# Dealing the experts' contraction rows so that each partition reads one contiguous 16 KB piece of every gate, up and down matrix

## The reference

```python
def moe_ffn(h, g_norm, wgr, bgr, wer, ber, wg, wu, wd):
    u = rms_norm(h, g_norm).reshape(n, d)                 # n = 264, d = 1024
    gates = route(u, wgr, bgr, wer, ber)                  # two of 16 experts per token, others 0
    a = jnp.einsum('td,edf->tef', u, wg)                  # wg, wu: (16, 1024, 512) per layer
    c = jnp.einsum('td,edf->tef', u, wu)
    hh = jax.nn.silu(a) * c * gates[:, :, None]
    return h + jnp.einsum('tef,efd->td', hh, wd)          # wd: (16, 512, 1024) per layer
```

## Time and profile before

| | |
|---|---|
| median of 3 runs | 1362.0 us (1359.39 to 1366.07) |
| the profiled execution | 1360.1 us, of which the span of the trace is 1358.3 us |
| busy: TensorE matmul | 1150.4 us, 85% of the span |
| busy: TensorE weight load | 741.9 us, 55% |
| busy: VectorE, ScalarE, GpSimd | 421.2, 224.3 and 222.5 us |
| mean granted TensorE clock | 0.911 |
| DMA | 462.63 MB, mean 341 GB/s; SP's queue 88.5% of the 16 engines' span |

### The profile page before, as it was taken

How to read it: one execution, slowest core, us unless ns; L and a number is a source line. 1 busy time by engine, 2 the same in 40 slices (tenths; PEclk the granted TensorE clock), 3 DMA queues, 4 the chain that set the end, 5 groups by cost and what they waited for, 6 DMA issues and landing times.

```text
span 1358.3 us, 15981 instructions
## 1 busy us (share of the span) xinstructions
PE 1150.4 (85%) x5409; PEld 741.9 (55%) x5410; DVE 421.2 (31%) x821; ACT 224.3 (17%) x508; POOL 222.5 (16%) x466
## 2 busy tenths in 40 slices
PE   0899899999969999857898989888466989899888
PEld 0588688788723788744444444444354444444443
DVE  0354745845810575140111011112741111111112
ACT  0122122122100343111111111111011111111111
POOL 0002412411410121004012222100003122222100
PEclk9899999999967799965999999999665999999999
DMA  9999899999789988999999898998999898989997
GB/s 310 309 339 344 295 392 370 376 403 369 285 299 379 357 257 282 345 371 332 359 373 350 331 348 334 356 390 329 384 325 303 309 366 313 351 334 350 385 340 278
DMA packets 132562, 462.63 MB, mean 341 GB/s; under 512 B 12112, under 2 KB 20192, under 8 KB 129808
## 3 DMA queue, kind: packets, MB, share of 16 engines
q1 hardware_dynamic: 118768, 440.29, 88.5%
q0 software_dynamic: 5536, 18.88, 3.8%
q10 hardware_dynamic: 8232, 3.13, 1.0%
HBM read 455.19 MB, written 183.41 MB: 470 GB/s over the span
## 4 chain that ended last, share of the span: by engine, by line
PE 58%; DVE 8%; issue 5%; ACT 2%; POOL 1%; ACTq 1%; DMA 0%; POOLq 0%; DVEq 0%
PE bank L1192 17%; PE bank L1175 11%; PE bank L1208 8%; PE bank L1217 4%; PE bank L1130 2%; PE bank L1062 2%; PE bank L1089 1%; PE bank L1182 1%; PE bank L1109 1%; PE bank L1097 1%; PE bank L1139 1%; PE bank L278 1%; PE bank L1069 1%; PE bank L1086 1%; DVE scratch L929 1%
## 5 line engine op out<-in xcount | busy, mean ns | idle before, releaser
L1019 PE MATMUL bank<-uT,ring_lo 128*128 128x264 f32 x1152 | 275.0, 394 | 8.5 <-DVE uT L291 6.0
L1019 PEld LDWEIGHTS bank<-uT,ring_lo 128*128 128x128 f32 x1152 | 218.7, 194 | 49.2 <-issue 9.6
L1175 PE MATMUL bank<-scratch 128*128 128x128 f32 (+1 forms) x768 | 149.2, 328 | 40.3 <-POOL scratch L559 24.8
L1175 PEld LDWEIGHTS bank<-scratch 128*128 128x128 f32 (+1 forms) x768 | 113.9, 204 | 78.3 <-issue 28.0
L1192 PE MATMUL bank<-ring_lo,scratch 128*64 128x512 f32 x512 | 127.8, 657 | 0.0
L1208 PE MATMUL bank<-ring_lo,scratch 128*64 128x512 f32 x512 | 113.4, 594 | 11.5 <-DVE scratch L931 11.5
L763 DVE RECIPROCAL scratch<-scratch 128x264 f32<-128x264 f32 x48 | 86.5, 1802 | 108.5 <-ACT scratch L615 108.5
L929 DVE TENSOR_TENSOR scratch<-bank,scratch 128x512 f32<-128x512 f32 x16 | 11.1, 692 | 331.9 <-PE bank L1192 331.9
L1192 PE MATMUL bank<-region_a,scratch 128*64 128x512 f32 x512 | 112.6, 592 | 0.0
L934 DVE TENSOR_TENSOR hT<-bank,hT 128x264 f32<-128x264 f32 x128 | 55.4, 433 | 129.7 <-PE bank L1217 128.4
L1208 PEld LDWEIGHTS bank<-ring_lo,scratch 128*64 128x64 f32 x512 | 42.2, 137 | 72.3 <-issue 72.3
(11 more groups left out here) (218 smaller groups left out, 1204.2 us busy)
## 6 DMA issues: line engine op xcount, KB each, us to landing
out_dram<-in_cache_kv_w_dram SPq DMA_DIRECT2D x128, 1023.5 KB, 16.7
ring_lo<-in_w_gate_dram SPq DMA_DIRECT2D x32, 2048.0 KB, 13.5
region_a<-in_w_up_dram SPq DMA_DIRECT2D x32, 2048.0 KB, 17.9
ring_lo<-in_w_down_dram SPq DMA_DIRECT2D x32, 2048.0 KB, 17.0
ring_lo<-in_w_qkv_dram SPq DMA_DIRECT2D x18, 2048.0 KB, 13.6
out_dram<-in_cache_kv_w_dram SPq DMA_DIRECT2D x32, 1022.0 KB, 31.9
ring_lo<-in_cache_kv_w_dram POOLq DMA_DIRECT2D x24, 512.0 KB, 9.3
ring_lo<-in_cache_kv_w_dram SPq DMA_DIRECT2D x6, 2048.0 KB, 13.8
```

Source lines behind the costliest of these rows:

```text
L1019: last = mm(z_bank[s % 4][:, 0:T], w[:, k, at:at + P], uT[:, k, :], start=(k == 0), stop=(k == KT - 1))
L1175: last = mm(bank[m // 4][:, m % 4 * P:(m % 4 + 1) * P], u_tok[0:sizes[b], b, m * P:(m + 1) * P], pick[0:sizes[b], b, :], start=(b == 0), s ...
```

## The change

Row p*8+k of a gate or up matrix (p*4+k of down) now goes to partition p, piece k, so that a partition holds 8 (4) neighbouring rows, which lie together in DRAM: one piece of 16 KB. The slot holds them one after the other as before, and the matmuls read it by the same indices. What stands against them must be dealt the same way. For gate and up, group m of `u_tok` must hold features m, m+8, m+16, ...: the copies at L863 and L699 now read their PSUM bank with a step of 8 elements and write eight runs of 64. For down, transpose f takes `hid_rows` columns f, f+4, f+8, ..., a stationary operand with a step of 4 elements (16 bytes).

```diff
+        def dealt(b, half, n):
+            return u_tok[0:n, b, :].rearrange("t (k p) -> t k p", k=KT)[:, :, half * HD:(half + 1) * HD]
...
-        expert_w = (w_gate.rearrange("l e (k p) f -> (l e) p k f", p=P),
-                    w_up.rearrange("l e (k p) f -> (l e) p k f", p=P),
-                    w_down.rearrange("l e (k p) f -> (l e) p k f", p=P))
+        expert_w = tuple(w.rearrange("l e (a p k) f -> (l e) p a (k f)", a=1, p=P) for w in (w_gate, w_up, w_down))
...
-                sp.dma_start(slot(s).rearrange("p (k f) -> p k f", k=FT if what == 2 else KT), src).then_inc(ring_full[s], 16)
+                sp.dma_start(slot(s).rearrange("p (a f) -> p a f", a=1), src).then_inc(ring_full[s], 16)
...
-                    nc.scalar.activation(u_tok[0:n, b, D // 2:], bank[2 * b + 1][0:n, :], ACT.Copy).then_inc(u_tok_act, 1)
+                    nc.scalar.activation(dealt(b, 1, n), bank[2 * b + 1][0:n, :].rearrange("t (p k) -> t k p", k=KT), ACT.Copy).then_inc(u_tok_act, 1)
...
-                    vec.tensor_copy(u_tok[0:n, b, 0:D // 2], bank[2 * b][0:n, :]).then_inc(u_tok_dve, 1)
+                    vec.tensor_copy(dealt(b, 0, n), bank[2 * b][0:n, :].rearrange("t (p k) -> t k p", k=KT)).then_inc(u_tok_dve, 1)
...
-                    last = nc.tensor.transpose(bank[f // 2][:, f % 2 * P:(f % 2 + 1) * P], hid_rows[:, f * P:(f + 1) * P], ident[:])
+                    last = nc.tensor.transpose(bank[f // 2][:, f % 2 * P:(f % 2 + 1) * P], hid_rows[:, f::FT], ident[:])
```

## The result

The changed kernel takes 1368.84 us in the median (1363.71 to 1372.39, 20 runs) against 1363.72 us (1359.39 to 1367.66, 20 runs) of before on the same chip. The ratio is 1.0035, with a 95% interval of 1.0023 to 1.0046: it is slower by 4.8 us, between 3.1 and 6.3. The profiled execution took 1371.6 us, its span 1369.8 us, so it is one of the slower ones. Two single executions in the record, 2917 us of the kernel before and 3890 us of the kernel with one more transpose, stand far from all others and are left out of every ratio.

What follows compares the result with a forecast made beforehand. TensorE was taken to bound the kernel, with the expert loads hidden. Loads 0, transposes 4.5, copies 0.5 and clock 0 made 5.0 us on 1362.0: 1367.0, shaded to 1366 us, range 1357 to 1376.

Steps and rivals of the forecast that it cites:

- What bounds the kernel: Whole kernel: TensorE is 58% of the chain, DMA 0%; expert loads are hidden with 3.4 us to spare per round.
- The loads: Six expert loads per round: 16 KB pieces make them 3 to 6% shorter, but nobody waits, so 0 us gained.
- F: Time that one expert round's transfers take: 35.8 us of the 39.2 us that the round lasts.
- The transposes: Four per expert round, strided operand: 0.07 us more per load, 4.5 us in all, between 0 and 9.0.
- rule on lines of 16 bytes: Strided transposes: SBUF needs two hits per 16-byte line for full bandwidth; by it their cost lies at the upper end, 9.0 us.
- The copies to u_tok: Copies from PSUM with a step of 8, before the router in each layer: 0.5 us in all, between 0 and 1.1.
- The granted clock: Gate and up matmuls at TensorE's lower clock in every second round: 0 us change for rounds 0.3 us longer.
- rival of the full penalty: Strided transposes cost a full loading time or more, with one to three more clock drops: 1373 us, chance 0.25.
- drops: Stretches with TensorE granted 1.2 GHz, 1.6 us each, in 7 of 14 rounds; two allowed to either side, 3.2 us.

Runs made afterwards that it cites:

- dealt product: The changed kernel with contiguous transposes again, VectorE dealing the features by reading both product inputs at a step of 4 elements: 1376.79 us, ratio 1.0094.
- reordered kernel with two more transposes: The kernel before with the six place matmuls run during ScalarE's copy and two more contiguous transposes per round: 1351.32 us, ratio 0.9909.

## Why the prediction was right, and where its sum was not

*What bounds the kernel* held: the loads were hidden, and the kernel with the 16 KB pieces alone, at 0.9992, shows that making them faster gives nothing. One row was misread: the 385.2 us in which SP waits are for the gate and the up matmuls, both of line 1192, and not for the gates alone, and they did not stay as they were but grew to 434.9.

*The loads* were sized too small. I expected 1 to 2 us off F and it was 3.7. The rate rose by 6 to 9% and not by 3 to 6, and gates and downs landed 2.4 us sooner each. It changed nothing, since nobody waits for them. The idle stretch of the DMA engines grew to about 6 us, the upper end of the forecast's 4 to 6.

*The transposes.* The price of a single load was right, 0.072 us where I had taken 0.070. The step that failed is "they go at the pace of the loads and all that a load gains or loses is on the path". The timelines say why; first four loads and four matmuls of before, then of after:

```profile
1103.54 0.42 PEld L1197 LDWEIGHTS bank<-ident,scratch 128*128 128x128 f32 x4 [1.75 <-DVE scratch L929]
1103.54 0.66 PE L1197 MATMUL bank<-ident,scratch 128*128 128x128 f32 x4 [0.86 <-DVE scratch L929]
```

```profile
1108.95 0.56 PEld L1200 LDWEIGHTS bank<-ident,scratch 128*128 128x128 f32 x4 [1.74 <-DVE scratch L932]
1108.95 0.75 PE L1200 MATMUL bank<-ident,scratch 128*128 128x128 f32 x4 [0.86 <-DVE scratch L932]
```

Four loads of 0.14 us fill only 0.42 us, and four of 0.21 only 0.56: they overlap one another, and the overlap grows with their length. Between the first and the second matmul of the four lie 0.16 us before and 0.22 after, but between the others 0.11 and 0.12. On the path came 0.09 us per round, not 0.28: 1.5 us in all where the sum had 4.5.

The rule on lines of 16 bytes in the Trainium skill's page "SBUF — State Buffer" (section "Door 1: The DMA port swizzle") held in its direction, and here its price is half a contiguous load more on TensorE. It did not bring the sum to its upper end, as the prediction took it to say.

*The copies to u_tok* cost 0 and not 0.5 us. A step of 8 elements in PSUM is free for VectorE (690 ns) and ScalarE (597 ns).

*The granted clock* was the term I set to 0 for a shift of up to 0.3 us per round. The shift was 0.09 and the term was the larger part of the loss: 4.8 - 1.5 = 3.3 us, by subtraction, between 1.6 and 4.8 by the interval. So the sum of 5.0 us (4 in the forecast, which was shaded) met 4.8 by luck: two terms missed by 3 us each, in opposite directions. The direction and the place of the loss were right for the reason given, its size was not. That a lengthening costs more than itself was in the prediction only inside the rival of the full penalty.

How much is shown: that the loss comes from the strides in TensorE's operand (the transposes alone slow it, dealing by ScalarE undoes it, the loads alone do nothing); that 1.5 us of it is direct; that lengthening a round at the same place by other means costs about 8 us for 2 and for 4; that the drops hang on the gaps before and after the gather, since four of the six kernels with a gap filled or removed have a profile without one behind the first round of a layer. Argued, not shown, is that the clock takes all of the other 3.3 us. The single profiles of the strided kernel and of that with one more transpose have the 7 drops of before. The changed kernel and the dealt product show one long stretch of low clock over a whole gather, which costs 4.4 to 4.9 us there; if it came in the 11 of 20 runs with a low mean clock, that would be 2.4 to 2.7 us on average (an estimate from these numbers).

## What to carry to other kernels

A load that lands 13 us before its use is worth nothing when it gets faster; look first at who waits, and then at what the new layout costs the engines that do wait. If a layout needs a stride somewhere, put it where it is free (here a read of PSUM by ScalarE or VectorE), not into an operand in SBUF on the path. And on a path bound by TensorE, the gaps of under a us can be worth more than their length: taking out one of 0.75 us per round, 0.9% of the time by itself, gave 1.2 to 1.6%.

## What the runs showed of the hardware that I had not expected

- A stationary operand with a step of 16 bytes loads in 212 ns instead of 140; four of them and their matmuls take 0.76 us and not 0.67.
- VectorE's product of 512 columns takes 692 ns with one input at a step of 4 elements in PSUM, and 1048 ns when the input in SBUF has that step too.
- With pieces of 16 KB per partition a load stream runs at 431 to 434 GB/s, with 4 KB at 409, with 2 KB at 397, and SP issues two loads of ups in 0.8 us instead of 5.2.
- Two matmuls of 512 columns per round that compute nothing made a kernel bound by TensorE 0.65% faster; its clock stayed at 2.4 GHz in every round that is not the first of a layer.
- The lower clock can also last over a whole gather of 48 matmuls, which then takes 13.0 to 13.4 us and not 8.5; it did so in one profile of the changed kernel, of the dealt product and of the reordered kernel with two more transposes.
